# A two-layer hybrid encoder step: the first and the last norm reordered, and the attention units taken in turn

## The chip, the cores and the metric

The kernel runs on one core of one Trainium2 chip. The metric is the device time of one execution in microseconds (us). Five engines work side by side, each through its own list of instructions in order: TensorE (PE) multiplies and transposes, VectorE (DVE) and ScalarE (ACT) do elementwise work and reductions, GpSimd (POOL) does slower elementwise work, and SyncE (SP) issues most DMA transfers. They wait for each other through semaphores that are written out by hand.

## The reference

One step over nine tiles of 128 rows: tiles 0 to 7 are a new prompt of 1024 frames, tile 8 holds 8 running streams of 16 frames with caches. Each of two layers computes

```python
h = rmsnorm(x) ; z = h @ W_in              # columns of z split among three kinds of heads
A = forgetting attention                   # "fox": 4 heads x 64, causal, logits plus a cumulated log-forget term
B = latent attention                       # "mla": 8 heads, low-rank q and kv, rotary part of 32, chunk mask
C = sliding window with sinks              # "swa": 4 query heads, window 128, relative bias
x = x + concat(A, B, C) @ W_out
x = x + square(relu(rmsnorm(x) @ W_up)) @ W_down
```

and after both layers a final RMSNorm with gain `g_final` gives `y_prompt` and `y_sample`. A softmax row is `exp(s - max)/sum`; in the sliding kind a learned sink joins maximum and sum.

## The kernel before, in words

Every engine's program is one function in one `Block`. All large products are split into a high and a low part: ACT casts to the high part (`in_hi`, `hi`), DVE or POOL subtracts to get the low part (`lo`).

**Start.** SP loads four constants, x tiles 0 and 1, the cosines, the gain `g1_bc` and the first two weight pieces (`w_raw`). A piece i+2 is loaded only when the low part of piece i is made. PE makes the relative-bias table in banks 0 to 3 (L2048), ACT scales it into `skew` (L1132), stores it (L1135), issues the loads of x tiles 2 to 8 (L1137), and only then takes the sums of squares of tiles 0 and 1 (`norm1`, L1152). POOL turns each into a reciprocal root (`norm_row`, L948/L949), but between tiles 1 and 2 it makes the low parts of weight pieces 2 and 3 (L959). DVE scales the row (`scale_row`, L1572), PE transposes it (L2068), ACT makes the high part (L1215), DVE the low part (L1583), and PE starts the input product. x is also stored to a DRAM scratch and read back before the output product.

**Prompt attention.** The work is a list `UNITS`. A unit is some heads of one kind for one tile of queries, as many as fit 1024 columns of scores; "q1" is the product for the latent queries of a tile, "q2" their transposition. The list runs tile by tile: q1, two forgetting units, q2, the other forgetting units, the sliding unit, then all latent units. Every engine walks it in steps of one unit: at step i PE transposes the probabilities of unit i-3, computes the scores of unit i and, where a group of heads ends at unit i-4, its product with the values; DVE copies the even chunks of transposed probabilities (L1686), normalises unit i-2 (L1695, L1698), and takes the maxima of unit i: for latent units a reduction (L1723), for the others one operation that adds the table, writes the logits and gives the maximum (L1730). A small instruction (L1737) turns the maximum into the negative bias of the exponential, and at the end of the step DVE copies the head outputs out of PSUM (L1747). ACT takes the exponentials (L1296), the odd chunks (L1275), and copies the queries (L1281, L1285). The last of these steps also hold the transposition of `wukv` and the latent queries of the streams (L2213, L2220, copy L1304). SP loads the caches of the streams once the last forgetting or sliding unit has its maxima (`NFOX_SWA_END`).

**End.** When the last residual additions (DVE, L1989 and L1995) are done, the final norm goes tile by tile over three engines: ACT squares into PSUM (L1551), POOL takes the reciprocal root (L1114, L1117), ACT scales (L1555), POOL multiplies by the gain (L1123), for tiles 0 to 6 (`POOL_Y = 7`); for tiles 7 and 8 DVE does both factors in one instruction (L2041). SP stores each tile.

## Time and profile before

| | us |
|---|---|
| median of 3 runs | 2891.95 (2887.72 to 2896.25) |
| the profiled execution | 2892.33 |
| its span | 2890.5 |
| PE busy | 2743.0 (95%) |
| DVE busy | 1789.4 (62%) |
| ACT busy | 1055.8 (37%) |
| POOL busy | 1054.9 (36%) |
| chain that ended last: PE, DVE, issue | 82%, 9%, 3% |
| mean granted TensorE clock | 0.985 |

The span is what the rows show, from the first instruction to the last; 1.83 us of the execution's time lie around it. PE is busy nearly everywhere, so the busy shares in 40 slices matter most where they are not 9: the first slice (7), the slices of the prompt attention and the last slice (5).

### The profile page before, as it was taken

What the parts mean: (1) busy time and instruction counts of PE and PEld (TensorE: products, weight loads), DVE (VectorE), ACT (ScalarE), POOL (GpSimd) and SP (SyncE); (2) the same over time, 40 slices, a digit from 0 to 9 for tenths busy, and PEclk for the clock granted to TensorE, in tenths of its full rate; (3) what the DMA queues carried; (4) which work ended last, traced back from release to release, by engine and by line L of the source; (5) the groups of instructions that cost most, each with busy time, mean ns of one, the idle gap of its engine ahead of it and who ended that gap; (6) DMA issues with size and microseconds to landing.
All of it is one profiled execution on the core that took longest, in us unless ns stands there. A gap on an engine that the chain in (4) does not pass through costs nothing.

```text
span 2890.5 us, 39775 instructions
## 1 busy us (share of the span) xinstructions
PE 2743.0 (95%) x14966; PEld 2214.5 (77%) x14966; DVE 1789.4 (62%) x2451; ACT 1055.8 (37%) x1877; POOL 1054.9 (36%) x581
## 2 busy tenths in 40 slices
PE   7998999899999999999999989999999999999995
PEld 5986666687888887888789766667878888788884
DVE  3126887734564558888730478875365455788884
ACT  3225544423333232333332354443252333333333
POOL 2111000014544456777511200000155444577775
PEclk9999999999999999999999999999999999999997
DMA  5111001432333456344131200023423333744331
GB/s 205 56 35 47 24 17 42 134 128 99 120 128 130 151 183 235 126 141 132 57 116 56 52 17 17 16 72 104 160 81 140 139 146 116 277 156 141 128 115 73
DMA packets 165539, 311.64 MB, mean 108 GB/s; under 512 B 24832, under 2 KB 90528, under 8 KB 165408
## 3 DMA queue, kind: packets, MB, share of 16 engines
q1 hardware_dynamic: 161088, 302.80, 30.4%
q10 hardware_dynamic: 4320, 7.08, 0.7%
q8 instruction: 84, 1.38, 0.2%
q14 instruction: 47, 0.39, 0.0%
HBM read 207.40 MB, written 102.44 MB: 107 GB/s over the span
## 4 chain that ended last, share of the span: by engine, by line
PE 82%; DVE 9%; issue 3%; ACT 2%; POOL 2%; DMA 1%; ACTq 0%; SPq 0%; DVEq 0%; POOLq 0%
PE ps L2533 7%; PE ps L2537 7%; PE ps L2535 7%; PE ps L2443 7%; PE ps L2444 7%; PE ps L2445 7%; PE ps L2204 5%; PE ps L2058 5%; PE ps L2056 5%; PE ps L2057 5%; PE ps L2234 4%; PE ps L2257 3%; PE ps L2319 2%; PE ps L2173 1%; PE ps L2388 1%
## 5 line engine op out<-in xcount | busy, mean ns | idle before, releaser
L2533 PE MATMUL ps<-wq_hi,sa_hi 128*128 128x512 f32 x896 | 350.8, 392 | 5.3 <-DVE x L1989 5.3
L2535 PE MATMUL ps<-wq_lo,sa_hi 128*128 128x512 f32 x896 | 350.5, 391 | 0.0
L2537 PE MATMUL ps<-wq_hi,sa_lo 128*128 128x512 f32 x896 | 350.1, 391 | 0.0
L959 POOL TENSOR_TENSOR w_lo<-w_raw,w_hi 128x1024 fp32r<-128x1024 f32 (+2 forms) x32 | 70.7, 2214 | 646.8 <-ACT w_hi L1149 646.8
L1989 DVE TENSOR_TENSOR x<-ps,x 128x1024 f32<-128x1024 f32 x224 | 264.3, 1212 | 56.9 <-PE ps L2537 54.7
L1927 DVE TENSOR_TENSOR sa_lo<-ra,sa_hi 128x1024 fp32r<-128x1024 f32 x112 | 281.2, 2512 | 24.3 <-ACT sa_hi L1419 24.2
L1034 POOL TENSOR_TENSOR wq_lo<-wsum,wq_hi 128x1024 fp32r<-128x1024 f32 x64 | 157.2, 2458 | 291.1 <-ACT wq_hi L1399 291.1
L2056 PE MATMUL ps<-w_hi,hT_hi 128*128 128x512 f32 (+2 forms) x672 | 248.5, 370 | 0.1
L2058 PE MATMUL ps<-w_hi,hT_lo 128*128 128x512 f32 (+2 forms) x672 | 246.2, 366 | 0.0
L2057 PE MATMUL ps<-w_lo,hT_hi 128*128 128x512 f32 (+2 forms) x672 | 245.1, 365 | 0.0
L1919 DVE TENSOR_TENSOR cq<-ps,cq 128x1024 f32<-128x1024 f32 x48 | 58.6, 1222 | 286.4 <-ACT cq L1460 244.2
L1040 POOL TENSOR_TENSOR wq_lo<-bsum,wq_hi 128x1024 fp32r<-128x1024 f32 x64 | 171.2, 2685 | 114.6 <-ACT wq_hi L1410 114.6
L2443 PE MATMUL ps<-hT_hi,wq_hi 128*128 128x512 f32 x512 | 202.5, 396 | 6.8 <-DVE hT_lo L1883 6.8
L1040 POOL TENSOR_TENSOR wq_lo<-rq,wq_hi 128x1024 fp32r<-128x1024 f32 x64 | 168.6, 2645 | 98.4 <-ACT wq_hi L1410 98.4
L2533 PEld LDWEIGHTS ps<-wq_hi,sa_hi 128*128 128x128 f32 x896 | 169.2, 189 | 42.1 <-issue 6.1
L2445 PE MATMUL ps<-hT_hi,wq_lo 128*128 128x512 f32 x512 | 200.7, 392 | 0.0
L2444 PE MATMUL ps<-hT_lo,wq_hi 128*128 128x512 f32 x512 | 200.6, 392 | 0.0
L2537 PEld LDWEIGHTS ps<-wq_hi,sa_lo 128*128 128x128 f32 x896 | 169.3, 189 | 35.6
L2535 PEld LDWEIGHTS ps<-wq_lo,sa_hi 128*128 128x128 f32 x896 | 169.3, 189 | 34.8
L1034 POOL TENSOR_TENSOR wq_lo<-rq,wq_hi 128x1024 fp32r<-128x1024 f32 x64 | 170.4, 2673 | 57.8 <-ACT wq_hi L1399 57.3
L1460 ACT COPY cq<-ps 128x512 f32<-128x512 f32 x128 | 73.3, 587 | 277.7 <-PE ps L2445 161.3
L2234 PE MATMUL ps<-identF,pbuf 128*128 128x128 f32 x984 | 140.4, 281 | 29.7 <-DVE pbuf L1698 27.5
(326 smaller groups left out, 6321.4 us busy)
## 6 DMA issues: line engine op xcount, KB each, us to landing
ra<-hidden_scratch SPq DMA_DIRECT2D x112, 512.0 KB, 3.4
hidden_scratch<-cq SPq DMA_DIRECT2D x94, 512.0 KB, 2.7
rq<-in_w_up_dram SPq DMA_DIRECT2D x64, 512.0 KB, 3.9
rq<-in_w_down_dram SPq DMA_DIRECT2D x64, 512.0 KB, 4.3
residual_scratch<-x SPq DMA_DIRECT2D x36, 512.0 KB, 5.0
x<-residual_scratch SPq DMA_DIRECT2D x36, 512.0 KB, 7.5
w_raw<-in_w_in_dram SPq DMA_DIRECT2D x16, 512.0 KB, 4.9
mixer_scratch<-omixT SPq DMA_DIRECT2D x16, 512.0 KB, 2.8
```

The lines of the kernel that those rows point to most:

```text
L1034: nc.gpsimd.tensor_tensor(wq_lo[o % 4][:], up_source(o)[:], wq_hi[o % 4][:], ALU.subtract).then_inc(up_lo.sem, 1)
L1040: nc.gpsimd.tensor_tensor(wq_lo[k][:], down_b_source(o)[:], wq_hi[k][:], ALU.subtract).then_inc(b_lo.sem, 1)
L1927: nc.vector.tensor_tensor(low.rearrange("p k n -> p (k n)"), raws, high.rearrange("p k n -> p (k n)"), ALU.subtract).then_inc(a_lo.sem, 1)
L2056: pe.matmul(out, ah, bh, start=(k == 0), stop=False)
L2057: pe.matmul(out, ah, bl, start=False, stop=False)
L2058: last = pe.matmul(out, al, bh, start=False, stop=(k == n - 1))
L2443: pe.matmul(out, wh[:, cols], h[:, k, :], start=new and k == 0, stop=False, skip_group_check=True)
L2444: pe.matmul(out, wh[:, cols], lo_h[:, k, :], start=False, stop=False, skip_group_check=True)
L2445: last = pe.matmul(out, wl[:, cols], h[:, k, :], start=False, stop=k == 3, skip_group_check=True)
L2533: pe.matmul(out, ah[:, k, :], bh[:, k * 512:(k + 1) * 512], start=new and k == 0, stop=False, skip_group_check=True)
L2535: pe.matmul(out, ah[:, k, :], bl[:, k * 512:(k + 1) * 512], start=False, stop=False, skip_group_check=True)
L2537: last = pe.matmul(out, al[:, k, :], bh[:, k * 512:(k + 1) * 512], start=False, stop=final and k == 1, skip_group_check=True)
```

## The change

The list of units takes half the forgetting units, a quarter of the latent units, q1 of the *next* tile, a quarter, the sliding unit, a quarter, the other forgetting units, q2 of the next tile, and the last quarter. The latent queries are copied times `-SCALE_M`, tables and sinks are used with turned sign, and minima are taken, so that the minimum itself is the bias and L1737 goes. The head outputs are copied by ACT at the end of its step. At the start SP issues all x tiles, the cosines later; the bias table uses banks 4 to 7 and is scaled after the first two weight pieces; layer 0 doesn't store x, and reads it back from the input. At the end ACT only squares, into SBUF, POOL only makes roots, DVE multiplies all nine tiles in the order `LAST_TILES`.

```diff
-POOL_Y = 7
+LAST_TILES = (0, 1, 2, 3, 8, 4, 5, 6, 7)
+def halves(units, parts):
+    n = (len(units) + parts - 1) // parts
+    return [units[i * n:(i + 1) * n] for i in range(parts)]
-UNITS = []
+UNITS = [("q1", 0, 0, 0)]
 for _t in range(NPT):
-    _rest = [("q1", _t, 0, 0)] + _fox[:2] + [("q2", _t, 0, 0)] + _fox[2:] + _swa
...
-    UNITS += _rest + tile_units("mla", _t)
+    _f0, _f1 = halves(tile_units("fox", _t), 2)
+    _m0, _m1, _m2, _m3 = halves(tile_units("mla", _t), 4)
+    if _t == 0:
+        UNITS += _f0 + [("q2", 0, 0, 0)]
+        _f0 = []
+    UNITS += _f0 + _m0 + [("q1", _t + 1, 0, 0)] + _m1 + tile_units("swa", _t) + _m2 + _f1 + [("q2", _t + 1, 0, 0)] + _m3
```

The start, on SP:

```diff
-            for t in range(2):
-                load(x[:, t, :], xp[t], x_in[t])
-            load(cs[:], c["cos_sin"], cs_in)
+            load_first((0, 1))
...
                 for j in range(4):
                     piece(j, in_piece(l, 0, j))
-                sp.wait_ge(dn_ev.sem, dn_ev.at(l * NS, 0))
-                for t in range(NT):
-                    sp.wait_ge(x_in[t].sem, x_in[t].at(l, 0))
-                    load(xs_d[t], x[:, t, :], xs_out)
+                    if l == 0 and j == 1:
+                        load_first((2, 3))
+                if l == 0:
+                    load_first(range(4, NT))
+                    load(cs[:], c["cos_sin"], cs_in)
+                else:
+                    sp.wait_ge(dn_ev.sem, dn_ev.at(l * NS, 0))
+                    for t in range(NT):
+                        sp.wait_ge(x_in[t].sem, x_in[t].at(l, 0))
+                        load(xs_d[t], x[:, t, :], xs_out)
```

The start, on ACT (the scaling and its store now stand behind `norm1(0)`, `norm1(1)`, `in_hi(0)` and `in_hi(1)` of layer 0):

```diff
-            nc.scalar.mul(skew[:], ps[:, 0:2048].rearrange("p (h n) -> p h n", h=SWA_H)[:, :, 0:384],
-                          8.0).then_inc(pro.sem, 1)
-            act.dma_start(skew_h.ap(), skew[:]).then_inc(skew_out.sem, 16)
-            for t in range(2, NT):
-                act.dma_start(x[:, t, :], xp[t] if t < NPT else xs).then_inc(x_in[t].sem, 16)
```

The attention steps, ACT's first and DVE's behind them:

```diff
-                            nc.scalar.copy(qTm[t % 2][0:QK_M], S[0:QK_M, :].rearrange("p (h n) -> p h n", h=MLA_H)
+                            nc.scalar.mul(qTm[t % 2][0:QK_M], S[0:QK_M, :].rearrange("p (h n) -> p h n", h=MLA_H),
+                                          -SCALE_M if t < NPT else 1.0).then_inc(sm_done.sem, 1)
...
+                    if i >= LAG and group_ending(i - LAG) is not None:
+                        act.wait_ge(pv_mm.sem, pv_mm.at(l, n + 1))
+                        nc.scalar.copy(omixT[t % 2][:, c0:c0 + pairs, :].rearrange("p k n -> p (k n)"),
+                                       bank(6 + n % 2)[:, 0:pairs * P]).then_inc(o_ev.sem, 1)
...
-                                chain.link(nc.vector.tensor_reduce(m, scores, AX_X, ALU.max))
+                                nc.vector.tensor_reduce(nm, scores, AX_X, ALU.min).then_inc(max_done.sem, 1)
...
-                                        SCALE64, -3e38 if kind == "fox" else sink_bc[:, h:h + 1], ALU.add, ALU.max,
-                                        mx[:, n % 4, g:g + 1])
+                                        -SCALE64, 3e38 if kind == "fox" else nsink[:, h:h + 1], ALU.add, ALU.min,
+                                        negm[:, n % 4, g:g + 1])
-                            nc.vector.tensor_scalar(nm, m, -SCALE_M if kind == "mla" else -1.0,
-                                                    None, ALU.mult).then_inc(max_done.sem, 1)
-                        nc.vector.tensor_copy(omixT[t % 2][:, c0:c0 + pairs, :].rearrange("p k n -> p (k n)"),
-                                              bank(6 + n % 2)[:, 0:pairs * P]).then_inc(o_ev.sem, 1)
```

The end, on POOL, ACT and DVE:

```diff
-                    nc.gpsimd.tensor_tensor(x[:, t, :], x[:, t, :], gF_bc[:], ALU.mult).then_inc(fin["yF_pool"].sem, 1)
...
-                act.wait_ge(dn_ev.sem, x_done(DEPTH, NPT if t < 4 else t))
-                nc.scalar.activation(bank(2 * (t % 2), 2), x[:, t, :], ACT.Square, scale=D ** -0.5,
-                    nc.scalar.mul(x[:, t, :], x[:, t, :], rstd[:, t:t + 1]).then_inc(fin["xF_scaled"].sem, 1)
+                act.wait_ge(dn_ev.sem, x_done(DEPTH, t))
+                nc.scalar.activation(cq[n % 2][:], x[:, t, :], ACT.Square, scale=D ** -0.5,
...
+                            if last and l == DEPTH - 1 and unit == 7 and pair == 0:
+                                last_norm(0)
...
+            for n in range(1, NT):
+                last_norm(n)
```

**The order on PE, tile 7 of the prompt.** `identF,pbuf` is a transposition of probabilities, `qkTf,qzf` are forgetting scores, `qkTs,qzs` sliding scores, `kTm,qTm` latent scores, `wuq,latT` is q1 and `identF,qtok` q2. In the program before, from the last forgetting unit on:

```order
L2204 MATMUL ps<-qkTf,qzf_206 128x512 x2
L2206 MATMUL ps<-cmaskB,identB 128x128
...
L2234 MATMUL ps<-identF,pbuf_181 128x128 x8
L2204 MATMUL ps<-qkTs,qzs_208 128x256 x4
L2180 MATMUL ps<-identF,qtok 96x128 x8
L2234 MATMUL ps<-identF,pbuf_182 128x128 x8
L2204 MATMUL ps<-kTm,qTm_198 128x512 x2
L2234 MATMUL ps<-identF,pbuf_179 128x128 x8
L2204 MATMUL ps<-kTm,qTm_198 128x512 x2
```

The same place in the changed program, from the latent unit ahead of the sliding one:

```order
L2221 MATMUL ps<-kTm,qTm_199 128x512 x2
L2221 MATMUL ps<-qkTs,qzs_209 128x256 x4
...
L2251 MATMUL ps<-identF,pbuf_180 128x128 x8
L2221 MATMUL ps<-kTm,qTm_199 128x512 x2
...
L2221 MATMUL ps<-qkTf,qzf_207 128x512 x2
L2223 MATMUL ps<-cmaskB,identB 128x128
L2251 MATMUL ps<-identF,pbuf_180 128x128 x8
L2197 MATMUL ps<-identF,qtok 96x128 x8
L2251 MATMUL ps<-identF,pbuf_181 128x128 x8
L2221 MATMUL ps<-kTm,qTm_199 128x512 x2
```

Sliding scores and q2 no longer stand side by side: between them are latent and forgetting units. The last unit that isn't latent is now the fourth from the end of the list (forgetting, q2, two latent ones); it was the tenth (sliding, q2, eight latent ones).

**The order on SP, the start.** Before:

```order
L635 DMA x<-in_x_prompt_dram 128x1024 x2
L635 DMA cs<-const_cos_sin_dram 128x288
L635 DMA g_bc<-in_g_attn_dram 128x1024
L635 DMA w_raw_61<-in_w_in_dram 128x2x512
L635 DMA w_raw_62<-in_w_in_dram 128x2x512
L635 DMA w_raw_61<-in_w_in_dram 128x2x512
L635 DMA w_raw_62<-in_w_in_dram 128x2x512
```

And in the changed program:

```order
L642 DMA x<-in_x_prompt_dram 128x1024 x2
L642 DMA g_bc<-in_g_attn_dram 128x1024
L642 DMA w_raw_61<-in_w_in_dram 128x2x512
L642 DMA w_raw_62<-in_w_in_dram 128x2x512
L642 DMA x<-in_x_prompt_dram 128x1024 x2
L642 DMA w_raw_61<-in_w_in_dram 128x2x512
L642 DMA w_raw_62<-in_w_in_dram 128x2x512
L642 DMA x<-in_x_prompt_dram 128x1024 x4
L642 DMA x<-in_x_sample_dram 128x1024
L642 DMA cs<-const_cos_sin_dram 128x288
```

The seven loads of x that ACT issued now stand in SP's queue, two of them behind the first two weight pieces and the rest behind the next two.

**The order on DVE, the end.** Before, the last rows are

```order
L1995 TENSOR_TENSOR x<-ps,x 128x512
L1989 TENSOR_TENSOR x<-ps,x 128x2x512 x2
L2041 SCALAR_TENSOR_TENSOR x<-x,rstd,gF_bc 128x1024 x2
```

and in the changed program

```order
L2011 TENSOR_TENSOR x<-ps,x 128x512
L2005 TENSOR_TENSOR x<-ps,x 128x2x512
L1586 SCALAR_TENSOR_TENSOR x<-x,rstd,gF_bc 128x1024
L2005 TENSOR_TENSOR x<-ps,x 128x2x512
L1586 SCALAR_TENSOR_TENSOR x<-x,rstd,gF_bc 128x1024 x8
```

One of the nine norms stands ahead of the last residual addition, eight behind it.

## Rows read from the trace of the kernel before

**Rows 1.** The chain that ended last, first 33 us: start, us, what.
```profile
9.96 1.46 ACT skew L1132
21.51 5.17 DMA w_raw<-in_w_in_dram
27.89 4.73 POOL w_lo L959 x2
```

**Rows 2.** Timeline at the start: start, us, engine, what [idle before <- releaser].
```profile
4.39 0.33 SPq L635 DMA_DIRECT2D g_bc<-in_g_attn_dram  x1
16.81 1.03 ACT L1152 ACTIVATE ps<-x 128x1024 f32<-128x1024 f32 x1 [5.40 <-issue]
18.91 1.98 ACT L1149 CAST w_hi<-w_raw 128x1024 fp32r<-128x1024 f32 x2
20.27 2.48 DVE L1578 TENSOR_TENSOR w_lo<-w_raw,w_hi 128x1024 fp32r<-128x1024 f32 x2
```

**Rows 3.** DMA: issues between 4.2 and 12 us, size, us to landing; then two of the whole span.
```profile
w_raw<-in_w_in_dram SPq DMA_DIRECT2D x2, 512.0 KB, 8.5
g_bc<-in_g_attn_dram SPq DMA_DIRECT2D x1, 512.0 KB, 7.2
...
w_raw<-in_w_in_dram SPq DMA_DIRECT2D x8, 416.0 KB, 3.3
```

**Rows 4.** The end: timeline of DVE and POOL.
```profile
2845.50 1.23 DVE L1989 TENSOR_TENSOR x<-ps,x 128x1024 f32<-128x1024 f32 x1 [1.50 <-PE ps L2537]
2856.38 1.23 DVE L1989 TENSOR_TENSOR x<-ps,x 128x1024 f32<-128x1024 f32 x1 [1.50 <-PE ps L2537]
2886.20 1.28 DVE L2041 SCALAR_TENSOR_TENSOR x<-x,rstd,gF_bc 128x1024 f32<-128x1024 f32 x1 [0.44 <-POOL rstd L1117]
2859.43 2.34 POOL L1123 TENSOR_TENSOR x<-x,gF_bc 128x1024 f32<-128x1024 f32 x1 [1.26 <-ACT x L1555]
2863.80 2.34 POOL L1123 TENSOR_TENSOR x<-x,gF_bc 128x1024 f32<-128x1024 f32 x1 [1.26 <-ACT x L1555]
```

**Rows 5.** DMA in the window 20 to 32 us.
```profile
DMA packets 1556, 4.73 MB, mean 394 GB/s; under 512 B 145, under 2 KB 145, under 8 KB 1556
```

**Rows 6.** Stretches of prompt attention: us, busy PE, PEld, DVE, ACT, POOL, clock, DMA, GB/s.
```profile
244.00:276.00 32.00, 25.45 (x174) 19.59 (x176) 21.95 (x91) 17.58 (x63) 3.25 (x8) 1.00 0.05 18
276.00:350.00 74.00, 71.00 (x526) 47.91 (x521) 60.48 (x185) 37.87 (x108) 3.17 (x8) 1.00 0.07 24
350.00:520.00 170.00, 162.64 (x1187) 110.55 (x1186) 137.04 (x347) 77.43 (x179) 3.28 (x8) 0.99 0.09 26
520.00:536.00 16.00, 13.70 (x152) 11.18 (x150) 7.79 (x16) 5.94 (x10) 0.00 (x0) 1.00 0.42 132
496.00:500.00 4.00, 4.00 (x13) 2.27 (x12) 2.80 (x7) 1.18 (x3) 0.00 (x0) 0.61 0.96 230
```

**Rows 7.** PE's waits, 244 to 536 and 1664 to 1956 us: total, times, longest.
```profile
PE ps L2234 <- DVE pbuf L1698: 13.8, 19, 2.3
...
PE ps L2234 <- DVE pbuf L1698: 13.7, 19, 2.2
```

**Rows 8.** Timeline from 491 us: DVE in the sliding unit, and PE's longest wait.
```profile
491.29 0.48 DVE L1730 CUSTOM_DVE_ANT_0 pbuf<-ps,bias,sink_bc 128x256 f32<-128x256 f32 x1 [1.22 <-PE ps L2204]
494.24 1.09 PE L2234 MATMUL ps<-identF,pbuf 128*128 128x128 f32 x8 [2.30 <-DVE pbuf L1698]
```

**Rows 9.** DVE's groups from 244 to 536 us: busy us, mean ns | idle before.
```profile
L1747 DVE COPY omixT<-ps 128x128 f32<-128x128 f32 (+2 forms) x48 | 15.8, 329 | 5.8 <-PE ps L2257 5.0
L1737 DVE TENSOR_SCALAR negm<-mx 128x1 f32<-128x1 f32 (+3 forms) x73 | 11.6, 158 | 2.2
```

**Rows 10.** SP's cache loads: first issue, last of the latent set; landing of that one.
```profile
493.36 3.97 SPq L635 DMA_DIRECT2D ckv_c<-in_cache_mla_ckv_dram  x8
499.61 1.34 SPq L635 DMA_DIRECT2D winM_f<-const_mask_window_dram  x1
...
winM_f<-const_mask_window_dram SPq DMA_DIRECT2D x1, 120.0 KB, 3.1
```

More of the change, by code:

```diff
@@ L256, in hybrid_step @@
         sink_bc = keep("sink_bc", [P, SWA_H])
+        nsink = keep("nsink", [P, SWA_H])
         sink_rows = keep("sink_rows", [P, 1])
@@ L628, in hybrid_step @@
         xs = a["x_sample"].rearrange("s q d -> (s q) d")
+        x_source = [xp[t] for t in range(NPT)] + [xs]
         block = ctx.enter_context(nc.Block())
@@ L635, in load, with load_first @@
                 sp.dma_start(dst, src).then_inc(sem.sem, 16)
-            for dst, src in ((identF, c["ident"]), (constA, c["cmask"]), (onehot, c["onehot"]),
-                             (relb, a["rel_bias"])):
+            for dst, src in ((relb, a["rel_bias"]), (onehot, c["onehot"]), (identF, c["ident"]), (constA, c["cmask"])):
                 load(dst[:], src, const_in)
-            for t in range(2):
-                load(x[:, t, :], xp[t], x_in[t])
-            load(cs[:], c["cos_sin"], cs_in)
+            def load_first(tiles):
+                for t in tiles:
+                    load(x[:, t, :], x_source[t], x_in[t])
+            load_first((0, 1))
             for name in ("11", "streams", "12", "22", "S1", "S2"):
@@ L2047, in _ @@
             for h in range(SWA_H):
-                last = pe.matmul(bank(h)[:, 0:384], relbb[:, h, :], onehot[:], start=True, stop=True)
+                last = pe.matmul(bank(4 + h)[:, 0:384], relbb[:, h, :], onehot[:], start=True, stop=True)
             last.then_inc(pro_tab.sem, 1)
```

111 lines of the change are left out of this document (54 added, 57 removed).

## The prediction, made before the changed kernel was run

> **What bounds the kernel now.** I read the page's 40 slices first, then a table of stretches, then the chain of waits and the timeline of the places where PE is not full. PE is busy 95% of the span and its matmuls are the same before and after (the order of PE holds the same products), so the change can only give back time in which PE waits, or runs slowly. Three places hold nearly all that it touches. At the start PE does no product of the layer for 25 us. In the prompt attention PE is busy 25.45 of 32 us in the first two tiles, 71.00 of 74, 162.64 of 170 and 13.70 of 16 while it drains [rows 6]: 6.55 + 3.0 + 7.36 + 2.3 = 19.2 us idle in a layer of 292 us, and layer 1 has the same waits [rows 7]. At the end DVE's last wait for PE is over at 2856.38 [rows 4], and the span goes on to 2890.5.
>
> **The end: what the norm costs.** The last residual addition ends at 2856.38 + 1.23 = 2857.6. Before, a tile takes a round over ACT and POOL: two of POOL's gain products start 4.37 us apart (2859.43 and 2863.80, with 2.34 us of work and 1.26 us of waiting for ACT's scaling in each) [rows 4]. That goes on for seven tiles, DVE's last instruction ends at 2886.20 + 1.28 = 2887.5, and the last store lands at 2890.5, 3.0 us later [rows 4]. In the changed program ACT only squares, 1.03 us per tile [rows 2] and a short readout, POOL only takes roots, and DVE does both factors in 1.28 us [rows 4]. DVE is then the slowest of the three. Its first norm fits ahead of the last addition: tile 0 is complete with the addition of 2845.50, long before [rows 4], and in its 1.50 us of waiting 1.28 fits, so it costs nothing; without that cover it would cost at most 1.28. Eight norms remain: 8 x 1.28 = 10.2 us, to 2867.9. What is late next are the stores: eight tiles of 0.524 MB at 394 GB/s, the mean of a full stretch of transfers in this trace [rows 5], take 10.6 us from about 2859, which ends at 2870 with the first one's delay, beside 2867.9 + 3.0 = 2870.9. I take 2871, a gain of 19.5 us. Bounds: 18 if each norm has 0.2 us between instructions, 20.5 if eight of them overlap as the additions do.
>
> The Trainium skill says something against this: its page DMA: Bandwidth & Descriptors, section Where 436 GB/s comes from, holds that between HBM and SBUF about 358 GB/s bind. The row with 394 GB/s, a mix of stores and loads, stands above it. By the page the eight stores would take 11.7 us, and the end would come about 1.3 us later; by the row they just keep up with DVE.
>
> **The start.** ACT waits 5.40 us in its own issuing of seven x loads before its first square at 16.81 [rows 2], and before that for the bias table, whose scaling ends at 11.4 [rows 1]. The data is there much sooner: the gain is issued at 4.39 and lands 7.2 later, at 11.6 [rows 2, 3]; the first two weight pieces land 8.5 after their issue, some 13.3 [rows 3]; both queue behind 144 KB of cosines, which now go later, some 0.4 us. So the row of tile 0 can be scaled from 11.2, before ACT's first square in the program before, and the weights decide: high part of piece 0 at about 12.9 to 13.9, its low part 1.24 (half of 2.48) [rows 2] to 15.2. That is 6.3 us ahead of the 21.51 at which the next piece was issued [rows 1]. This piece then took 5.17 us beside x loads and x stores; now the nine stores are gone, x tiles 2 and 3 are ahead of it and five tiles behind it. A load of 416 KB takes 3.3 elsewhere [rows 3]; I take 3.4 for it: 18.6. High part 1.0, then POOL's two low parts 4.73 [rows 1]: 24.4, instead of 27.89 + 4.73 = 32.6. POOL's root for tile 2 and so PE's second tile wait for exactly that, so the gain is 8.2; I take 8. ACT's path in parallel (two high parts to 15, the table's scaling 1.46 [rows 1], its store's issue, the high part of the hidden tile to about 17.9) is ready before 18.6 and costs nothing; if the weights came 2 us sooner it would be the next bound. Bounds: 5.5 (piece 2 takes its 5.17 again and ACT is late by 1) to 9.5. Moving the cosines costs nothing, as DVE first needs them at the rotation of the keys, after four weight slabs.
>
> **The attention.** DVE loses two kinds of instructions: 73 negations a layer, 11.6 us, and 48 head copies, 15.8 us [rows 9], 27.4 of its 227 us there; ACT, at 139 of 292 us, takes the copies. PE isn't DVE's prisoner throughout, so this is not the gain; the gain is in PE's waits for normalised probabilities, 13.8 us in 19 places [rows 7]. The longest one, 2.30 us at 494.24, shows why: sliding scores and then q2, whose product is short and gives DVE no cover while it takes the sliding unit's four maxima (0.48 each, from 491.29) before it can normalise the next unit [rows 8]. In the new order a latent unit stands before and behind the sliding one, and q2 and its consumer are two units apart. After this wait the granted clock is 0.61 over 4 us [rows 6], which costs 4 x 0.39 = 1.6 us. I give back: of the 7.36 us 3.5, because after the sliding unit its own normalisation (four pieces) now comes with a latent maximum in front and about 0.9 us of waiting a tile will remain; of 3.0 us 1; of the first 6.55 0.5, since q1, a forgetting unit and q2 stand there as before and the first latent unit must wait for the copied queries; of the drain nothing; the shorter way from maximum to exponential (0.16 us a unit) is in these numbers; and 1.6 for the clock. Sum 6.6, taken as 7 a layer, 14 for both. Bounds per layer: -2 (new waits, nearest row 19.2 us idle in all for the size that such waits can have) to 12.
>
> One more wait moves: SP loads the caches when the last forgetting or sliding unit has its maxima. Before, that was 493.36, 42.6 us before the streams begin at 536; 12 steps lie between, 3.55 us each. Six of them go: 21.3 us remain. The latent set is complete at 499.61 + 1.34 + 3.1 = 504.05, 10.7 us after its first issue [rows 10]. It stays hidden by 10.6 us, and costs nothing until it is worth three more steps.
>
> **Sum.** 8 + 19.5 + 14 = 41.5. The profiled execution took 2892.33 (span 2890.5 and 1.83 around it), 0.4 above the median shown, so both serve alike: 2892.3 - 41.5 = 2851.
>
> **Rivals.**
> (B) The attention gives nothing: each wait removed comes back elsewhere, since three engines still follow one list in step and DVE's work per unit is uneven. For it: DVE is busy 60.48 of 74 and 137.04 of 170 us [rows 6], so it is near PE. Against it: 27 us less work on DVE. Time: 2892.3 - 27.5 = 2865.
> (C) The attention becomes PE-bound: 17 of 19.2 us and the clock's 1.6 come back in each layer, less the drain: 2892.3 - 27.5 - 34 = 2831. Against it: the first two tiles, where units are short and latencies rule.
> (D) Slower: the head copies now stand in ACT's list behind the exponentials, and wait for a product that PE makes after the scores. If ACT stands there while DVE's next maximum is ready, every later exponential is late, and PE two units later. It decides from 27.5/96 = 0.29 us lost per copy; at 0.6 us it would be 57.6 - 27.5 = 30 us slower, 2922. For it: no engine but ACT can hold both the exponential and the copy. Against it: ACT is busy only 77.43 of 170 us [rows 6], and PE makes the product while DVE still takes the maximum of the same step, so it should be there when ACT's exponential is over.
> (E) The weights don't land earlier, or POOL's low parts are late again: the start gives 3 instead of 8: 2856.
> (F) Stores at less than the 394 GB/s of a mixed stretch hold the end back by 1.5 us: 2852.5; this is the page's rule, told above.
>
> **Chances.** Forecast 0.57 (2843 to 2860); B 0.20; C 0.08; D 0.03; E 0.07; F 0.05. The range is 2838 to 2867: start 5.5 to 9.5, end 18 to 20.5, attention nearly nothing to 24, and B inside it. A measurement of this kernel tells about 0.3%, 9 us, from no change. Faster 0.94 (everything but D and a B with attention losing 18 us), same 0.03, slower 0.03.
>
> **What would show it.** The end: DVE's norms 1.3 us apart from about 2857.6 on the old scale, and a tail of 14 to 15 us behind PE's last product instead of 34. The start: POOL's low parts of the third and fourth piece 8 us sooner. The attention: no wait of over 1.5 us at q2, DVE at about 200 of a stretch of 285 us, a clock of 1.00 there. I am wrong if the attention stretch (first q1 product to latent queries, 292 us) isn't shorter by 4 us or more, if PE waits for ACT in it, or if the stores end over 4 us after DVE.

## The result, and the profile after

The changed kernel takes 2874.8 us (median of 5 runs, 2873.4 to 2879.8), the kernel before on the same chip 2890.5 (5 runs, 2887.7 to 2896.3). The ratio is 0.9944, 95% interval 0.993 to 0.9958: faster by 0.56%, some 16 us, where 41.5 were forecast. It lies above the range that was given, 2838 to 2867. The profiled execution took 2873.4, its span 2871.6, 18.9 less than before.

From the page of the changed kernel, the engines and the chain that ended last:

```profile
PE 2744.5 (96%) x14966; PEld 2217.5 (77%) x14966; DVE 1753.4 (61%) x2216; ACT 1069.8 (37%) x1968; POOL 1040.9 (36%) x574
...
PE 83%; DVE 9%; issue 3%; ACT 2%; POOL 1%; DMA 1%; SPq 0%; DVEq 0%; ACTq 0%; POOLq 0%
```

DVE lost 36 us of work and ACT gained 14, as the change says. Where the time went shows in the timeline of PE. I cut it at the first product of q1 and at the first transposition of `wukv`, which stands at the end of the attention's list (this stretch is 285.6 us before; the 292 of the prediction reached from 244 to 536). The changed kernel in both layers:

```profile
237.98 2.82 PE L2190 MATMUL ps<-wuq,latT 128*128 128x384 f32 x8 [0.77 <-ACT Vm L620]
...
530.23 1.04 PE L2230 MATMUL ps<-identF,wukv 128*128 128x128 f32 x8
...
1659.44 2.82 PE L2190 MATMUL ps<-wuq,latT 128*128 128x384 f32 x8 [0.77 <-ACT Vm L620]
...
1950.99 1.04 PE L2230 MATMUL ps<-identF,wukv 128*128 128x128 f32 x8
```

The kernel before at the same four places:

```profile
244.29 2.82 PE L2173 MATMUL ps<-wuq,latT 128*128 128x384 f32 x8 [0.77 <-ACT Vm L614]
...
529.92 1.04 PE L2213 MATMUL ps<-identF,wukv 128*128 128x128 f32 x8
...
1664.35 2.82 PE L2173 MATMUL ps<-wuq,latT 128*128 128x384 f32 x8 [0.77 <-ACT Vm L614]
...
1950.09 1.04 PE L2213 MATMUL ps<-identF,wukv 128*128 128x128 f32 x8
```

| us | before | after | difference | forecast |
|---|---|---|---|---|
| to the first q1 | 244.3 | 238.0 | -6.3 | -8 |
| attention, layer 0 | 285.6 | 292.3 | +6.6 | -7 |
| between | 1134.4 | 1129.2 | -5.2 | 0 |
| attention, layer 1 | 285.7 | 291.6 | +5.8 | -7 |
| the rest, to the end of the span | 940.4 | 920.6 | -19.8 | -19.5 |

Each kernel was profiled once, so a row of this table is one execution of each. How far a stretch moves by itself can be read from the kernels below: in those with the same start as the changed kernel the first q1 comes at 236.1 to 237.6 us. This profile's 238.0 is the latest of them.

**The end** came as forecast. DVE and SP, to be held against [rows 4]:

```profile
2855.44 1.28 DVE L1586 SCALAR_TENSOR_TENSOR x<-x,rstd,gF_bc 128x1024 f32<-128x1024 f32 x1
...
2856.74 11.42 SPq L642 DMA_DIRECT2D out_dram<-x  x9
2857.02 1.22 DVE L2005 TENSOR_TENSOR x<-ps,x 128x1024 f32<-128x1024 f32 x1 [0.30 <-PE ps L2554]
2858.16 9.64 DVE L1586 SCALAR_TENSOR_TENSOR x<-x,rstd,gF_bc 128x1024 f32<-128x1024 f32 x8
```

One norm hides in the wait ahead of the last addition, which shrinks from 1.50 to 0.30 us, and eight follow at 1.2 us each (9.64 us in all). DVE ends at 2867.8, the span 3.8 us later. The stores keep up, as two stretches of nothing but stores show (the last two columns are the DMA share and GB/s):

```profile
2862.00:2866.00 4.00, 0.00 (x0) 0.00 (x0) 4.00 (x4) 0.00 (x0) 2.54 (x3) 0.50 1.01 406
2866.00:2871.00 5.00, 0.00 (x0) 0.00 (x0) 1.80 (x2) 0.00 (x0) 0.00 (x0) 0.50 0.95 375
```

The 406 GB/s stand above the 358 that the Trainium skill (DMA: Bandwidth & Descriptors, section Where 436 GB/s comes from) gives as the bound between HBM and SBUF. The page and the measurement differ, and the measurement decides.

**The start** gave 6.3 us. ACT's high part of the fourth weight piece and POOL's low part behind it:

```profile
16.28 0.38 ACTq L1220 DMA_DIRECT2D bias_skew_scratch<-skew  x1
...
22.96 1.05 ACT L1151 CAST w_hi<-w_raw 128x1024 fp32r<-128x1024 f32 x1 [3.39 <-DMA w_raw<-in_w_in_dram]
...
24.09 2.36 POOL L973 TENSOR_TENSOR w_lo<-w_raw,w_hi 128x1024 fp32r<-128x1024 f32 x1 [2.00 <-ACT w_hi L1151]
```

POOL ends at 26.45, against 32.62 before and 24.4 forecast. The third piece came as forecast (ACT's high part of it starts at 18.53, forecast 18.6). The fourth didn't: ACT waits 3.39 us for it, and POOL stands still for 2.00 us between its two low parts, which the forecast had back to back.

**The attention** lost time, half of it as waits and half as slower work. These are the stretches of the table, layer 0, before and after (us, then the busy time of PE, PEld, DVE, ACT and POOL, the clock, DMA share and GB/s):

```profile
244.29:529.92 285.63, 267.80 (x1972) 184.75 (x1973) 226.52 (x636) 136.79 (x354) 9.69 (x24) 0.99 0.10 31
...
237.98:530.23 292.25, 271.17 (x1972) 188.05 (x1973) 204.74 (x515) 146.97 (x402) 9.57 (x24) 0.98 0.08 25
```

PE's idle time grows from 17.8 to 21.1 us, by 3.3, and its busy time by 3.4 for the same products. PE's waits in layer 0 (releaser, total, times, longest), to be held against [rows 7]:

```profile
PE ps L2251 <- DVE pbuf L1723: 15.3, 23, 3.0
PE ps L2221 <- ACT qTm L1293: 2.4, 1, 2.4
PE ps L2197 <- DVE qtok L1738: 1.7, 1, 1.7
PE ps L2251 <- ACT ptb L1283: 1.5, 3, 0.6
```

The timeline of tile 0 (PE, and ACT and DVE where they release it) shows the two long ones:

```profile
243.79 1.05 PE L2197 MATMUL ps<-identF,qtok 128*96 128x128 f32 x8 [1.72 <-DVE qtok L1738]
...
245.98 0.19 ACT L1304 ACTIVATION_READ_ACCUMULATOR pbuf<-pbuf,negm 128x1 f32 x1
246.07 1.00 ACT L1293 ACTIVATE qTm<-ps 96x1024 f32<-96x1024 f32 x1
...
247.22 3.75 PE L2221 MATMUL ps<-kTm,qTm 104*128 104x128 f32 x16 [2.38 <-ACT qTm L1293]
...
256.29 0.29 DVE L1733 TENSOR_TENSOR ropet<-qtok,cs 128x128 f32<-128x128 f32 x1 [3.46 <-ACT qtok L1289]
...
258.31 1.66 DVE L1723 TENSOR_SCALAR pbuf<-pbuf,rinv 128x128 f32<-128x128 f32 x8
...
260.02 1.49 PE L2251 MATMUL ps<-identF,pbuf 128*128 128x128 f32 x8 [3.04 <-DVE pbuf L1723]
```

The latent unit stands directly behind q2. Its scores need the queries that ACT copies, and ACT has the forgetting unit's exponentials ahead of the copy. Two units later, DVE stands still for 3.46 us waiting for the copy of q1(1), and the normalisation that PE waits for is behind that in DVE's list. The granted clock (third column from the right) around it, in pieces of 2 us:

```profile
244.00:246.00 2.00, 0.84 (x8) 0.58 (x6) 0.48 (x6) 1.48 (x8) 0.00 (x0) 1.00 0.00 0
246.00:248.00 2.00, 0.78 (x4) 0.81 (x5) 1.05 (x5) 1.07 (x3) 0.00 (x0) 0.73 0.00 0
248.00:250.00 2.00, 2.00 (x11) 2.00 (x11) 0.00 (x0) 0.00 (x0) 0.00 (x0) 0.50 0.00 0
250.00:252.00 2.00, 2.00 (x10) 1.96 (x10) 0.99 (x1) 0.00 (x0) 0.00 (x0) 0.50 0.00 0
252.00:254.00 2.00, 2.00 (x5) 1.00 (x4) 0.83 (x2) 1.73 (x10) 0.00 (x0) 0.56 0.00 0
254.00:256.00 2.00, 2.00 (x11) 1.31 (x10) 0.00 (x0) 1.72 (x9) 0.00 (x0) 1.00 0.00 0
...
260.00:262.00 2.00, 1.98 (x12) 1.94 (x13) 1.66 (x10) 0.72 (x4) 0.00 (x0) 0.64 0.00 0
262.00:264.00 2.00, 2.00 (x10) 1.59 (x8) 1.11 (x6) 2.00 (x9) 0.00 (x0) 0.50 0.00 0
```

Behind each wait the clock falls to its lower level, 1.2 of 2.4 GHz. The lost shares sum to 0.54 + 1 + 1 + 0.88 + 0.72 + 1 = 5.1 us. That is the most it can have cost, since PE partly waited in these pieces. Layer 1 has the same drops, at 1666 to 1674 and 1680 to 1684 us, behind waits of 1.72, 2.38 and 2.65. Before, this place had 1.00 throughout [rows 6] and only the drop at 496 us, 1.6, which is gone. The difference, 3.5 us, is about the growth of PE's busy time.

### The profile page after: what moved, and what is told of

It reads as the page before. It is cut to its first block, busy times and chain, and to the rows that moved or that the text cites. A ratio compares the mean times of both kernels' runs of the same rounds, so it can differ in the third digit from the quotient of the medians.

```text
span 2871.6 us, 39614 instructions
## 1 busy us (share of the span) xinstructions
PE 2744.5 (96%) x14966; PEld 2217.5 (77%) x14966; DVE 1753.4 (61%) x2216; ACT 1069.8 (37%) x1968; POOL 1040.9 (36%) x574
## 4 chain that ended last, share of the span: by engine, by line
PE 83%; DVE 9%; issue 3%; ACT 2%; POOL 1%; DMA 1%; SPq 0%; DVEq 0%; ACTq 0%; POOLq 0%
PE ps L2550 7%; PE ps L2552 7%; PE ps L2554 7%; PE ps L2460 7%; PE ps L2461 7%; PE ps L2462 7%; PE ps L2221 6%; PE ps L2073 5%; PE ps L2071 5%; PE ps L2072 5%; PE ps L2251 4%; PE ps L2274 3%; PE ps L2336 2%; PE ps L2190 1%; DVE pbuf L1723 1%
```

## The experiments

The time is the median of 4 to 12 executions, the stretch comes from the one that was profiled. "Stretch" is q1 to `wukv` as above, in layers 0 and 1. The kernels were timed on different chips, each beside the kernel before, so ratios are compared rather than times. Between executions of one kernel the time moves with the mean granted clock: e6 alone took 2854.5 us at 0.992 and 2862.0 at 0.988. So a difference of 2 us between two kernels, or a drop of the clock that one profile has, doesn't tell them apart.

| kernel | median us | ratio to before, 95% | stretch |
|---|---|---|---|
| before | 2890 to 2891 | 1 | 285.6, 285.7 |
| changed | 2874.8 | 0.9944 (0.993 to 0.9958) | 292.3, 291.6 |
| e1, old list | 2858.2 | 0.9883 (0.9863 to 0.9903) | 282.7, 282.3 |
| e2, new list alone | 2919.6 | 1.0103 (1.0079 to 1.0127) | 299.6, 299.4 |
| e3, copies on DVE | 2883.7 | 0.9976 (0.9962 to 0.999) | 295.8, 295.4 |
| e4, tiles 0, 1 old | 2863.7 | 0.9903 (0.9882 to 0.9923) | 286.9, 285.3 |
| e5, long fillers | 2883.6 | 0.9975 (0.9966 to 0.9984) | 294.2, 294.2 |
| e6, sign alone | 2860.1 | 0.9891 (0.9876 to 0.9906) | 284.8, 284.8 |
| e7, tile 0 swapped | 2869.2 | 0.9928 (0.9915 to 0.9942) | 287.2, 288.7 |
| e8, old list, q2 late | 2855.1 | 0.9882 (0.9867 to 0.9897) | 280.6, 280.3 |
| e9, short fillers | 2868.5 | 0.9917 (0.9902 to 0.9932) | 288.5, 288.5 |
| e10, x later | 2853.5 | 0.9865 (0.9846 to 0.9885) | 282.3, 281.9 |
| e11, table's store later | 2855.2 | 0.9875 (0.9856 to 0.9893) | 282.3, 280.3 |
| e12, tile 0 rearranged | 2857.0 | 0.9877 (0.9859 to 0.9895) | 283.0, 282.6 |
| e13, combined | 2852.0 | 0.9869 (0.9854 to 0.9884) | 280.7, 281.1 |
| e14, combined, fillers | 2851.2 | 0.9868 (0.9853 to 0.9883) | 280.7, 280.3 |
| e15, q1 moved | 2860.8 | 0.9897 (0.9882 to 0.9912) | 283.8, 283.8 |
| e16, sliding unit moved | 2869.7 | 0.9932 (0.9918 to 0.9945) | 288.1, 289.4 |

**Which part costs.** e1 is the changed kernel with the old `UNITS`:

```diff
-UNITS = [("q1", 0, 0, 0)]
+UNITS = []
...
-    UNITS += _f0 + _m0 + [("q1", _t + 1, 0, 0)] + _m1 + tile_units("swa", _t) + _m2 + _f1 + [("q2", _t + 1, 0, 0)] + _m3
...
+    _rest = [("q1", _t, 0, 0)] + _fox[:2] + [("q2", _t, 0, 0)] + _fox[2:] + _swa
...
+    UNITS += _rest + tile_units("mla", _t)
```

> The changed kernel with the old list of units; turned sign, head copies on ACT, new start and new end are kept. Theory 1 (the new order costs: waits in tile 0 and the low clock that follows them): the stretch from the first q1 product to the first latent queries of the streams is 287.8 us as before or a few us shorter, PE's granted clock from 240 to 270 us is 1.00, and the time is about 2861 (2874.8 less two times 6.8), within 2858 to 2864. Theory 2 (ACT's head copies cost, the order is neutral): the stretch stays near 294, time 2872 to 2877. Theory 3 (the one of the prediction: the order gives 7 us a layer and something else takes 13): the time rises to 2885 or more.

2858.2, stretch 9.6 and 9.2 us shorter than in the changed kernel, clock 1.00 in tile 0 of both layers. Theory 1 holds. e2 is the reverse of this diff, applied to the kernel before.

> The kernel before with the new list of units and nothing else changed. Theory 1: the stretch grows from 287.8 to 294 or more in each layer, with a granted clock of about 0.83 behind the first latent unit; time 2900 to 2907 against 2890.5 before. Theory 2: 2889 to 2893, since DVE still copies the heads. Theory 3: 2876 to 2884.

2919.6: 29 us slower than before, more than theory 1 said. The list costs 13.9 and 13.7 us with the old step and 9.6 and 9.2 with the new one. e3 is the changed kernel with the head outputs' copy, and its wait, at the end of DVE's step again:

```diff
-                        nc.scalar.copy(omixT[t % 2][:, c0:c0 + pairs, :].rearrange("p k n -> p (k n)"),
+                        nc.vector.tensor_copy(omixT[t % 2][:, c0:c0 + pairs, :].rearrange("p k n -> p (k n)"),
```

> The changed kernel with the head outputs copied by DVE again, new order and turned sign kept. Theory 1: the place of the copy hardly matters, 2873 to 2879, and the low clock behind tile 0's first latent unit is still there. Theory 2: 2859 to 2864.

3.5 and 3.9 us a layer and 9 in all slower, outside of what theory 1 gave: with the new list ACT's copies are a gain. Half of it is again the clock, which falls once more in this kernel (0.60 and 0.55 from 276 to 280 us, 1.7 us lost; as much at 1702 to 1708). e6 has the diffs of e1 and of e3 together.

> The kernel with the old list of units (2858.2) and the head outputs copied by DVE again: new start, new end and turned sign remain. The stretch is 285.6 in the kernel before and 282.7 with sign and ACT's copies. If the sign alone brings it (73 instructions off DVE's way from maximum to exponential), it stays near 283 and the time is 2858 to 2861. If the copies bring it, as they do in the new order (292.2 against 295.8 us), it returns to 285 to 286 and the time is 2863 to 2867.

The time, 2860.1, is the first answer's, the stretch, 284.8, nearer to the second's. By the stretches the copies are worth 2.1 and 2.5 us here (e6 against e1), the sign 0.8 and 1.0 (before against e6). The first is mostly clock: e6 has 0.63 and 0.51 from 259 to 263 us, 1.7 us lost, and as much in layer 1, and e1 has 1.00 there. The ratios, 0.9891 and 0.9883, don't tell e6 from e1, so with the old list a gain by the copies isn't shown.

**Where in the list.** e4 gives tiles 0 and 1 the old order:

```diff
+    if _t == 0:
+        UNITS += [("q1", 0, 0, 0)] + _fox + [("q2", 0, 0, 0)] + _swa + _mla
+        continue
+    if _t == 1:
+        UNITS += [("q1", 1, 0, 0)] + _fox + [("q2", 1, 0, 0)] + _swa + _mla[:1] + [("q1", 2, 0, 0)] + _mla[1:] + [("q2", 2, 0, 0)]
+        continue
```

> The changed kernel with the units of tiles 0 and 1 in the old order and those of tiles 2 to 7 in the new one. Theory 1: all of the loss sits in tile 0, so the stretch is 287 to 289 us, the granted clock in 240 to 270 us is 1.00, and the time is 2860 to 2864. It may be below the kernel with the old list by up to 2 us a layer (2 x 1.6), since the old order has a clock of 0.61 at 496 to 500 us which the new one has not. Theory 2: 2872 to 2877.

The time came as theory 1 said, and 5.4 and 6.2 us come back. The clock isn't 1.00 throughout, as theory 1 had it: from 256 to 262 us it is 0.92, 0.50 and 0.72, 1.7 us lost, in layer 0 alone. And the stretch isn't below that of e1: 4.2 and 3.0 us remain, so not all of the loss sits in tile 0. e7 changes tile 0 alone:

```diff
-        UNITS += _f0 + [("q2", 0, 0, 0)]
+        UNITS += _f0 + [("q2", 0, 0, 0)] + tile_units("swa", 0) + [("q1", 1, 0, 0)] + _m0 + [("q2", 1, 0, 0)]
+        continue
```

> The changed kernel with tile 0 alone put in another order: q1(0), forgetting, q2(0), sliding, q1(1), latent, q2(1) (the new list has q2(0), latent, q1(1), sliding, q2(1)). The first latent unit then has two other pieces of TensorE work between the copied queries and itself. If the new order's loss sits at this one place, the waits of 2.4 and 3.0 us and the low clock go: stretch 286 to 288, time 2862 to 2867. If the later interleaving costs the rest, it ends about 2 us a layer above the old list (2858.2), so not below 2862.

The clock is 1.00 from 237 to 283 us, and 5.1 us come back; in layer 1 it still falls once (0.51 and 0.63 from 1680 to 1684 us, 1.7 us lost), and 2.8 come back. A new wait of 2.54 us for ACT's exponentials takes a part, so 2869.2 is above what was expected.

**Wait or clock.** e5 puts products that nobody reads into the three waits:

```diff
+                def filler(count):
+                    for _ in range(count):
+                        pe.matmul(bank(7), latT[:, 2, 0:P], wukv[:, 0:4].rearrange("p h e d -> p (h e d)"), start=True, stop=True)
...
+                        if t == 0:
+                            filler(4)
                         pe.wait_ge(rope_ok.sem, rope_ok.at(l, t + 1))
```

> The changed kernel with products whose results nobody reads on TensorE inside the three long waits of tile 0: four of 128x512 ahead of q2(0), five ahead of the first latent unit, six ahead of the transposition of the second unit's probabilities (0.23 us each, so 0.9, 1.2 and 1.4 us of waits of 1.7, 2.4 and 3.0). The output is the same. They hide no wait; they only keep TensorE busy. If the clock that follows the idle time is what costs (5.1 us of the loss: granted clock 0.50 from 247 to 254 and from 261 to 264 us), the clock is 1.00 there, the stretch from first q1 to the wukv transposition falls from 292.2 to 287 to 288, and the time to 2863 to 2867. If only the waits cost, or the clock falls anyway, the stretch stays at 292 and the time at 2873 to 2876.

The time went up by 9, of which the two stretches hold 4.5. I had mis-sized the filler: one takes 0.91 us, not 0.23 (the first row is four of them, two records each). Its rows still tell something:

```profile
240.09 3.65 PE L2183 MATMUL ps<-wukv,latT 128*128 128x512 f32 x8
...
244.45 4.46 PE L2183 MATMUL ps<-wukv,latT 128*128 128x512 f32 x10
...
256.62 5.42 PE L2183 MATMUL ps<-wukv,latT 128*128 128x512 f32 x12
```

13.5 us of products against 7.1 of waits should make the stretch 6.4 longer, and it grew by 1.9 and 2.6, at a clock of 1.00. In e9 they are fewer (the third place is the same in both, ahead of the transpositions of the second unit):

```diff
-                            filler(4)
+                            filler(1)
...
-                            filler(5)
+                            filler(2)
...
-                        filler(6)
+                        filler(3)
```

> The changed kernel again with extra products in the three waits of tile 0, but only as many as fit: 1, 2 and 3 of 128x512 (0.91 us each in the trace of the run before, which had 13.5 us of them, more than the 7.1 us of waits, and a stretch of 294.2 us at a clock of 1.00). Now nothing is made longer. If the clock drop alone was worth 5.1 us a layer, the stretch is 292.2 - 5 = 287 to 288 and the time 2863 to 2867. If 1 product is not enough to keep the clock up in the first wait, a part of the drop stays: stretch 289 to 291. If the long fillers' result came by their extra time and not by the clock, it stays at 292.

Stretch 288.5 and time 2868.5, between the first answer and the second, so 3.8 and 3.1 us a layer for adding 5.8 us of work. The windows of e9:

```profile
243.00:249.00 6.00, 5.30 (x33) 3.97 (x34) 2.25 (x14) 2.56 (x9) 0.00 (x0) 1.00 0.01 3
249.00:255.00 6.00, 4.77 (x26) 2.87 (x25) 2.87 (x7) 3.59 (x17) 0.93 (x2) 1.00 0.00 0
```

The clock is up throughout tile 0, in both layers; the gain falls short of 5 also because new waits appear, such as 1.23 us for the exponentials. The low clock in tile 0 is thus shown to be worth 3 to 4 us a layer. That it stayed up by chance is unlikely: with the new list in tile 0 and no filler (the changed kernel, e2, e3) it fell there in all six layers that were profiled, with fillers (e5, e9) in none of four. The Trainium skill, TensorE: Matmul & The Clock Gate, section A second HAM failure mode: psum-queue depth-cycling, tells of a kernel in which frequent short idles between groups of products sent the clock back and forth; this trace agrees as far as that goes, with 1.72 and 2.38 us of waiting ahead of the drop.

**The place that the prediction aimed at.** e8 is e1 with q2 of the streams behind tile 7's first two latent units:

```diff
-        _rest.append(("q2", NPT, 0, 0))
+        UNITS += _rest + tile_units("mla", _t)[:2] + [("q2", NPT, 0, 0)] + tile_units("mla", _t)[2:]
+        continue
```

> The kernel with the old list (2858.2), with the one place changed that the prediction aimed at: q2 of the streams stands behind the first two latent units of tile 7 instead of directly behind the sliding unit. If q2's place is the cause of the wait of 2.17 us at 484.1 and of the low clock behind it (1.6 us), both go, 3 us a layer, and the time is 2851 to 2854. If the sliding unit's four pieces make the wait wherever q2 stands, 0.5 to 1 us goes and the clock stays 1.00 or not: 2855 to 2859.

In e1 the wait and its clock are still there, in the timeline

```profile
484.12 1.94 PE L2251 MATMUL ps<-identF,pbuf 128*128 128x128 f32 x8 [2.17 <-DVE pbuf L1723]
```

and the window behind it

```profile
485.00:487.00 2.00, 2.00 (x7) 1.48 (x7) 1.69 (x6) 1.78 (x4) 0.00 (x0) 0.50 0.85 246
```

In e8 they have shrunk or gone, in the timeline

```profile
484.32 1.09 PE L2252 MATMUL ps<-identF,pbuf 128*128 128x128 f32 x8 [1.32 <-DVE pbuf L1724]
...
487.50 1.09 PE L2252 MATMUL ps<-identF,pbuf 128*128 128x128 f32 x8 [0.38 <-DVE pbuf L1724]
```

and in the window

```profile
484.00:488.00 4.00, 3.31 (x17) 2.00 (x18) 3.93 (x10) 3.17 (x11) 0.00 (x0) 1.00 0.72 208
```

The stretches are 2.0 us shorter in both layers, nearly all of it clock: the wait falls from 2.17 to 1.70 in two pieces, and the drop behind it (as much in layer 1) is gone. The span of the profiled execution is 3.7 us shorter than that of e1. The medians don't show it: their ratios to before are the same, 0.9882 and 0.9883.

**The small waits from tile 2 on.** e15 and e16 take e8 and move one thing each. e15, q1 between latent units (`_k` is a quarter of the latent units, for tile 0 all of them):

```diff
+    UNITS += _fox[:2] + [("q2", _t, 0, 0)] + _fox[2:] + _swa + _mla[:_k] + [("q1", _t + 1, 0, 0)] + _mla[_k:]
```

> The kernel with the old list and a late q2 for the streams (e8: 2855, stretch 280.6 and 280.3), with q1 of tiles 2 to 7 alone moved to the place the new list gives it, between latent units of the tile before. If q1's six rotations (1.75 us of DVE), which then stand ahead of a latent unit's normalisation, make the new list's small waits, the stretch grows by 2 to 4 us a layer and the time is 2859 to 2863. If q1's place is harmless, within 1 us of 2855.

2860.8, stretch 3.1 and 3.5 longer, in the range of the first expectation. The clock stays at 1.00 in tile 0, as in e8, so this isn't the clock: PE waits for normalised probabilities 21 times, 13.0 us in all, in e8 16 times, 10.7. Its timeline shows how:

```profile
292.32 0.29 DVE L1733 TENSOR_TENSOR ropet<-qtok,cs 128x128 f32<-128x128 f32 x1 [1.67 <-ACT qtok L1289]
...
293.79 0.68 DVE L1711 COPY ptb<-ps 128x512 f32<-128x512 f32 x1
...
294.58 0.75 DVE L1723 TENSOR_SCALAR pbuf<-pbuf,rinv 128x384 f32<-128x384 f32 x2
...
295.38 0.87 PE L2251 MATMUL ps<-identF,pbuf 128*128 128x128 f32 x6 [0.81 <-DVE pbuf L1723]
```

DVE waits 1.67 us for the copy of q1, rotates, and only then normalises the unit that PE is ready for. e16, the sliding unit between latent units (`_k` is half of them, for tile 0 none):

```diff
+    UNITS += [("q1", _t, 0, 0)] + _fox[:2] + [("q2", _t, 0, 0)] + _fox[2:] + _mla[:_k] + _swa + _mla[_k:]
```

> The same kernel (e8) with the sliding unit of tiles 1 to 6 alone moved between latent units, as the new list has it. If the sliding unit between latent ones makes the small waits (0.4 and 0.25 us around it in the changed kernel), the stretch grows by 1 to 3 us a layer, 2857 to 2861. By the prediction (a latent unit's work covers the four sliding pieces) it gets shorter by 1 to 2 us a layer: 2851 to 2853. If both this and the run with q1 alone show nothing, the splitting of the forgetting units is what is left.

2869.7, stretch 7.5 and 9.0 longer, more than either side expected. The largest part is in tile 1, where the latent unit stands behind q2 again, and the copy is awaited again:

```profile
262.83 3.13 PE L2221 MATMUL ps<-kTm,qTm 104*128 104x256 f32 x8 [2.41 <-ACT qTm L1293]
```

After that the clock is 0.62 and 0.53 over 4 us, 1.7 us lost (3.4 in layer 1). The sliding unit behind q2 was the cover of the query copy, so this is a second case of tile 0's mechanism. The rest comes later. From the product of q1(2) on, both lists still take the tiles one by one, and both have a clock of 1.00. In e8 and in e16 it starts at

```profile
269.54 2.75 PE L2191 MATMUL ps<-wuq,latT 128*128 128x384 f32 x8
...
274.58 2.75 PE L2190 MATMUL ps<-wuq,latT 128*128 128x384 f32 x8
```

and the attention ends at 517.79 and 525.54: 248.3 us against 251.0, and 247.9 against 250.6 in layer 1. So the sliding unit between latent units costs 2.7 us a layer in tiles 2 to 6 as well, most of it in small waits (for normalised probabilities 7.9 instead of 7.1 us in layer 0, for ACT's odd chunks 2.2 instead of 1.6, for copied queries 0.6 more). That is what the first expectation said; the gain that the prediction counted on isn't there.

**Tile 0 once more.** e12 is e8 with another tile 0:

```diff
+    if _t == 0:
+        UNITS += [("q1", 0, 0, 0)] + _fox + _swa + [("q2", 0, 0, 0), ("q1", 1, 0, 0)] + tile_units("mla", 0)
+        continue
+    if _t == 1:
+        _rest = _rest[1:]
```

> The same fastest kernel with tile 0 in the order q1(0), forgetting, sliding, q2(0), q1(1), latent. The sliding scores (1.06 us) stand in the wait of 1.72 us ahead of q2(0), and the product of q1(1) (2.75 us) between the query copy and the latent unit. If the waits of tile 0 follow from what stands ahead of q2 and of the first latent unit, 1 to 2.5 us a layer go: stretch 278 to 279.6 instead of 280.6, time 2850 to 2853. If the chain q1, rotation, q2, copy only pushes its wait to the next unit (DVE has the sliding unit's maxima ahead of the rotation then), nothing or up to 1 us a layer is lost.

The stretch is 2.4 and 2.3 us longer, more than its rival had said: q2(0) now waits 1.9 us for DVE's maxima and q2(1) 0.8 for the exponentials, and the clock is 0.50 to 0.53 from 247 to 253 us. The profiled execution was the slowest of four (2861.1 us, the others 2856.2 to 2857.2), and the ratio, 0.9877, isn't above that of e8. So the expected gain isn't seen, and a loss isn't shown.

**The start.** Both from e8. e10:

```diff
-                    load_first(range(4, NT))
-                    load(cs[:], c["cos_sin"], cs_in)
+                    load_first((4,))
...
                     piece(4 + j, in_piece(l, 1, j))
+                if l == 0:
+                    load_first(range(5, NT))
+                    load(cs[:], c["cos_sin"], cs_in)
```

> The fastest kernel so far (old list, q2 of the streams late, 2855) with the loads of x tiles 5 to 8 and of the cosines issued behind weight pieces 5 and 6 instead of directly behind piece 4. The start was forecast to give 8 us and gave 6.3, because the fourth weight piece lands 6.6 us after its issue. If the x loads that are issued right behind it share its time, it lands 1.5 to 3 us sooner, POOL's second low part ends at 24 instead of 25.6, and the time falls by 1 to 2 us. If something else holds it (the store of the bias table, 768 KB, issued by ACT at the same time), nothing moves.

POOL's last low part starts at 23.30, in e8 at 23.23: the x loads aren't it. The first q1 comes 1.1 us sooner, at 236.0, but two kernels with the unchanged start have it at 236.1 and 236.2. e11 moves the store of the table into the loop behind `evac_z(1)`:

```diff
-                    act.wait_ge(pro.sem, 2)
-                    act.dma_start(skew_h.ap(), skew[:]).then_inc(skew_out.sem, 16)
...
+                    if t == 2 and l == 0:
+                        act.wait_ge(pro.sem, 2)
+                        act.dma_start(skew_h.ap(), skew[:]).then_inc(skew_out.sem, 16)
```

> The same fastest kernel with the store of the bias table (768 KB) issued by ACT behind the third tile's work, some 15 us later, instead of at about 15.5 us. If this store is what delays the weight pieces 3 and 4, they land 1.5 to 2.5 us sooner and the time falls by 1.5 to 2 us; if the x loads are it, nothing moves.

Here the fourth piece is there sooner:

```profile
20.84 1.05 ACT L1152 CAST w_hi<-w_raw 128x1024 fp32r<-128x1024 f32 x1 [1.78 <-DMA w_raw<-in_w_in_dram]
...
21.96 2.40 POOL L974 TENSOR_TENSOR w_lo<-w_raw,w_hi 128x1024 fp32r<-128x1024 f32 x1 [0.39 <-ACT w_hi L1152]
```

1.3 us sooner than in e8, and the first q1 comes 2.3 sooner, at 234.8. The median shows nothing of it (ratio 0.9875, e8 0.9882); a gain of this size is within its interval. The traces do: from ACT's first high part to its fourth it takes 10.1 to 11.1 us in all thirteen kernels that store the table there (e10 among them), and 8.9, 8.3 and 8.9 in the three that store it later (e11, e13, e14). The 768 KB of the table's store beside the weights hold the start back by at least 1.1 us.

**The best.** e13 has all three edits: e8's list, e10 and e11.

> What the runs so far point to, in one kernel: the changed kernel with the old list, q2 of the streams two latent units later, the store of the bias table issued some 15 us later, and x tiles 5 to 8 with the cosines behind weight pieces 5 and 6. If the delays of the fourth weight piece by the store and of the x loads add, it is 1 to 2 us below either: 2851 to 2854. If they are the same bandwidth, 2853 to 2856.

e14 adds to e13 the filler of e5, once in each of three places:

```diff
+                        if t == 0:
+                            filler(1)
                         pe.wait_ge(rope_ok.sem, rope_ok.at(l, t + 1))
...
+                    if n in (0, 2):
+                        filler(1)
                     pe.wait_ge(norm_ok.sem, norm_ok.at(l, n + 1))
```

> The same kernel with one unread 128x512 product (0.91 us) in each of the three waits of tile 0 that are 1.6 to 2.0 us long (ahead of q2(0), of the first and of the third unit's transpositions). Each fits into its wait. With the same waits the granted clock fell behind the third one in three kernels (0.5 over about 3.5 us) and didn't in two others. If a little work in the waits keeps it up, the clock is 1.00 in tile 0 in both layers, the stretch 280.5 in both, and the time 0 to 3 us less than without. If the clock falls anyway, no difference.

2852.0 and 2851.2: both beat the kernel before (1.3% below it) and the changed one, and they can't be told apart. Nor do their intervals part from those of e8, e10, e11 and e12, so what is shown is the step from the changed kernel to e1, not those behind it. The clock in tile 0 was 1.00 in both. Whether it falls there in layer 0 varies with nearly the same waits (it does for about 3.5 us in e4, e6, e10 and e11, not in e1, e8, e13 and e15), and e14 doesn't settle whether the filler prevents it. Whether this belongs to the kernel or to the execution is open as well, since each was profiled once.

## Why the prediction was wrong

- **The end, right.** 19.5 forecast, 19.8 measured, by the steps it named: one norm free, eight at 1.2, stores that keep up. It held in every kernel with the new end (920 to 924 us behind the second attention, 940 before).
- **The start, nearly right, one wait left out.** 6.3 instead of 8 in this profile, 6.7 to 8.2 in the eleven other kernels with the same start, so the sum was about right. Its step "High part 1.0, then POOL's two low parts 4.73" failed: it has both pieces there together. The third came as forecast, but the fourth left ACT waiting for 3.39 us and POOL for 2.00. The prediction counted the x stores that had gone and not the table's store, which the change itself moves beside these loads. e11 gives 1.3 us of it back.
- **The attention, wrong in sign, by 13 us a layer.** Forecast 7 less, measured 6.6 and 5.8 more. Two steps failed. The first is "of the first 6.55 0.5, since ... the first latent unit must wait for the copied queries". The wait is named there and not priced. It was 2.38 us, a second of 3.04 followed at the normalisation, and the clock fell behind both, by up to 5.1 us. e4, e7 and e9 show it: tiles 0 and 1 hold 5.4 and 6.2 of the 9.6 and 9.2 us that the list costs. The second is "of the 7.36 us 3.5". It looked at the place around which the change improves something, the sliding unit and q2 of the streams in tile 7 (in e8 2 us a layer of the profile, nearly all clock, not seen in the medians). It didn't look at q1, which the new list puts between latent units, where its rotation stands ahead of a normalisation: 3.1 and 3.5 us (e15). And a latent unit ahead of the sliding one isn't the cover that it was taken for: 2.7 us a layer more (e16). These two leave little for the splitting of the forgetting units, which wasn't tried.
- **Fewer instructions on DVE, right in direction.** Sign and copies gave 3.0 and 3.4 us with the old list, 7.3 and 7.8 with the new one (e2 against the changed kernel), of which part is the clock. Rival D has nothing for it: ACT's head copies wait 0.2 us in all, and e3 is slower.
- **The cache loads, right.** SP's first one starts at 515.60, 20.6 us before PE needs it at 536.24, where 21.3 were forecast, and nobody waits.
- **The signs named.** Two of the three for being wrong came: the stretch is longer, and PE waits for ACT in it (2.38 us). The third, late stores, didn't: 3.8 us behind DVE, with the limit put at 4.
- **The bounds.** Rival B had the attention at no gain, and the lower bound was 2 us lost a layer. The loss was three times that: 3.3 us more of idle time, with a longest wait of 3.04 us where it had been 2.30, and 3.4 us more for the same products at the lower clock, which the prediction counted only as something to be given back. No rival has this path.
- **The stores.** The slower of the two reckonings (11.7 us instead of 10.6) makes them 1.1 us longer. As the prediction ends them at 2870, ahead of DVE's 2870.9, the end would have moved by a few tenths, not by the 1.3 of the text and the 1.5 of rival F. The end came without either.
- **Not explained.** Between the two attentions the changed kernel needs 1129.2 us, all others 1131 to 1134. In the window 1500 to 1640 us its granted clock is 1.00 and that of before 0.98, with the same work. Nothing that was changed acts there. These 5 us are a third of the 16 that were measured, and luck as far as is known: without them the changed kernel would stand further from its forecast.

## What to carry to other kernels

A list that several engines walk in step is tuned at its shortest units first. For each product-and-copy pair (q1 and its rotation, q2 and its copy) ask which unit covers it, and don't let the consumer be the next one. Where PE waits twice in a few microseconds (here 1.7 and 2.4 us), price the clock behind it, not only the waits. When an order is changed together with a cheaper step, time the step with the old order: here it alone was worth 0.6% more than both together (0.9883 against 0.9944).
